# Value matmuls of the older unit ahead of the transposes of the newer one, in the units' loop of a hybrid decoder step

## What is computed

```python
# NSA mixer: three branches (compressed, selected, window), each a masked softmax attention
s = einsum('btghd,bngd->btghn', q, k) * scale
p = masked_softmax(s, mask)
o_branch = einsum('btghn,bngd->btghd', p, v)
o = g0 * o_cmp + g1 * o_slc + g2 * o_win
# DSA mixer: one branch, whose mask keeps the top-k keys of an indexer
o_d = einsum('btghk,btkgd->btghd', masked_softmax(q . k, top_k_mask), v)
# then both are gated, projected up, merged, projected out, added to x, and normed
```

## Time and profile before

| | |
|---|---|
| median of three runs | 699.51 us |
| the profiled execution: its own time | 697.51 us |
| its span, first to last instruction | 695.7 us |
| mean granted TensorE clock | 0.970 of full |
| PE busy over the span | 635.9 us (91%) |
| DVE busy over the span | 371.5 us (53%) |
| ACT busy over the span | 270.2 us (39%) |
| POOL busy over the span | 146.9 us (21%) |

### The profile page before, as it was taken

One profiled execution on the slowest core, in us unless ns is written; L12 is line 12 of the kernel. 1 busy time (PEld: TensorE's weight loads), 2 busy tenths in 40 slices (PEclk: granted clock), 3 DMA queues, 4 the chain that ended last, 5 costly groups with the idle time before them and its releaser, 6 DMA issues. The chain is left out here.

```text
span 695.7 us, 12691 instructions
## 1 busy us (share of the span) xinstructions
PE 635.9 (91%) x4400; PEld 498.4 (72%) x4400; DVE 371.5 (53%) x1001; ACT 270.2 (39%) x627; POOL 146.9 (21%) x216
## 2 busy tenths in 40 slices
PE   3979999998999978798989998999999999999990
PEld 1269676675776865464655667999999999987770
DVE  2044213969878358887787782444232623153536
ACT  5133233333231455666666672434222332221312
POOL 1013541260250434343434340000000000000001
PEclk9969999999999998999999999999999999999996
DMA  9943532322442352001300404235532324132003
GB/s 326 366 125 114 190 118 84 90 74 63 136 138 64 113 165 62 1 2 32 93 1 2 116 9 122 61 122 137 184 82 75 104 66 120 62 100 69 14 1 129
DMA packets 51807, 68.40 MB, mean 98 GB/s; under 512 B 5009, under 2 KB 34889, under 8 KB 51584
## 3 DMA queue, kind: packets, MB, share of 16 engines
q1 hardware_dynamic: 48496, 54.63, 26.3%
q10 hardware_dynamic: 1808, 6.31, 2.6%
q0 software_dynamic: 1440, 6.66, 2.4%
HBM read 62.99 MB, written 6.66 MB: 100 GB/s over the span
## 5 line engine op out<-in xcount | busy, mean ns | idle before, releaser
L1283 ACT ACTIVATE w_hi<-stage 128x1024 fp32r<-128x1024 f32 (+3 forms) x64 | 63.4, 990 | 195.5 <-PE psum L930 106.8
L1548 DVE TENSOR_TENSOR w_lo<-stage,w_hi 128x1024 fp32r<-128x1024 f32 x40 | 48.9, 1225 | 130.4 <-ACT w_hi L1283 127.0
L786 PE MATMUL psum<-w_hi,hT_hi 128*128 128x512 f32 (+7 forms) x240 | 84.7, 353 | 3.3 <-DVE hT_lo L1523 3.2
L788 PE MATMUL psum<-w_lo,hT_hi 128*128 128x512 f32 (+7 forms) x240 | 83.4, 348 | 0.0
L787 PE MATMUL psum<-w_hi,hT_lo 128*128 128x512 f32 (+7 forms) x240 | 83.3, 347 | 0.0
L762 POOL TENSOR_SCALAR prob<-prob,softmax_stats 128x31 f32<-128x31 f32 (+4 forms) x128 | 61.8, 496 | 86.5 <-DVE softmax_stats L1754 60.5
L711 POOL TENSOR_TENSOR w_lo<-stage,w_hi 128x1024 fp32r<-128x1024 f32 (+3 forms) x24 | 45.7, 1904 | 162.2 <-ACT w_hi L1283 162.2
L930 PE MATMUL psum<-hT_hi,w_hi 128*128 128x272 f32 x384 | 79.5, 288 | 0.0
L930 PE MATMUL psum<-hT_lo,w_hi 128*128 128x272 f32 x384 | 79.5, 288 | 0.0
L930 PE MATMUL psum<-hT_hi,w_lo 128*128 128x272 f32 x384 | 79.2, 288 | 0.0
L1416 ACT ACTIVATE prob<-psum,softmax_stats 128x31 f32<-128x31 f32 (+6 forms) x136 | 63.4, 466 | 26.1 <-DVE softmax_stats L1733 14.4
(11 more groups left out here) (295 smaller groups left out, 1132.0 us busy)
## 6 DMA issues: line engine op xcount, KB each, us to landing
stage<-in_w_in SPq DMA_DIRECT2D x14, 1024.0 KB, 5.1
stage<-in_w_ada SPq DMA_DIRECT2D x8, 1024.0 KB, 7.6
stage<-in_w_in SPq DMA_DIRECT2D x10, 512.0 KB, 5.3
stage<-in_w_out SPq DMA_DIRECT2D x4, 1024.0 KB, 5.0
staging<-in_x_prompt ACTq DMA_DIRECT2D x4, 512.0 KB, 5.8
qT_plain<-in_w_ada SPq DMA_DIRECT2D x2, 1024.0 KB, 10.8
qT_rot<-in_w_ada SPq DMA_DIRECT2D x2, 1024.0 KB, 12.3
cached<-in_cache_nsa_kv SPq DMA_DIRECT2D x32, 64.0 KB, 2.3
```

The costliest lines, as they stand in the source:

```text
L786: mm(out, left[0], right[0], start=first, stop=False, skip_group_check=True)
L788: return mm(out, left[0], right[1], start=False, stop=last, skip_group_check=True)
L1283: last = A(dst, src, ACT.Copy)
L1548: last = tt(dst, src, hi.bitcast(F32), ALU.subtract)
```

## The change

The two calls in the loop change places, so that turn i issues scores(i), values(i - 4), turn(i - 3). The two waits of `turn` for the copies of the unit before go, since values(i - 4), now ahead of it, waits for the same copies.

```diff
--- before.py
+++ after.py
@@ -1146,10 +1146,7 @@
                 src = prob[:, u % 4]
                 for g in range(2 if kind == "P" else 1):
                     pe.wait_ge(scaled, TURNS[u] + g + 1)
-                    if g and ORDP[u]:
-                        pe.wait_ge(pt_dve, ORDP[u])
-                    elif not g and ORD[u]:
-                        pe.wait_ge(pt_act, ORD[u])
+
                     if kind == "P" and b != CMP:
                         for n in range(unit[3] + 1):
                             last = pe.transpose(bank[4 + g][:, P * n:P * n + P], src[:, g, P * n:P * n + P], ident)
@@ -1219,10 +1216,10 @@
             for i in range(len(UNITS) + LAG + 3):
                 if i < len(UNITS):
                     scores(i)
+                if 0 <= i - LAG - 1 < len(UNITS):
+                    values(i - LAG - 1)
                 if 0 <= i - LAG < len(UNITS):
                     turn(i - LAG)
-                if 0 <= i - LAG - 1 < len(UNITS):
-                    values(i - LAG - 1)
                 turn_samples(i - LAG - 2)
```

## The result

The changed kernel takes 722.37 us (median of 4 runs, 715.99 to 725.16), against 699.87 us for the kernel before (4 runs). The ratio is 1.0317, with a 95% interval of 1.0241 to 1.0393. That is slower, as forecast, but by 22.5 us and not by 13.5, and above the range's upper end of 720.

What follows compares the result with a forecast made beforehand. TensorE leads the loop, VectorE and ScalarE close behind. Bare copies of 9.5 (NSA blocks), 1.1 (S units), 0.5 (DSA) and 2.5 us (loop's end) make 13.6; 697.51 becomes 711.1, and the median, 2.0 higher, 713; range 704 to 720.

Steps and rivals of the forecast that it cites:

- The move of the wait: TensorE's loop: the wait for copies isn't removed but moves from the transposes to the values, earlier by a set of values.
- The sum of bare copies: Loop: copy time with hand-overs beyond the covering scores, summed over units and the loop's end, 13.6 us.
- WIN t = 3 and t = 2: NSA blocks: loss where these units' copies outlast the scores four units later, 0.66 and 0.53 us.
- the loop's end: Last units, with no scores left to cover their copies: 2.5 us, less the wait already there.
- waits before scores: ScalarE's later copy delays the exponentials that scores wait for; this link stays shorter than the new turn: nothing.
- the clock's term: TensorE's granted clock in the loop: new gaps of at most 0.8 us each leave it unchanged; nothing in the sum.
- the stage behind the loop: After the loop: unchanged; the freed weight load moves with the loop's end and costs nothing.
- rival 3: Clock falls: small gaps bring half-speed stretches, each 1.2 us dearer; five more would give 719. Chance 0.11.
- the main case: Whole kernel: 13.6 us of bare copies, clock unchanged, giving 713 us. Chance 0.80.
- rival 1: Absorbed: loss falls where VectorE or ScalarE limits anyway; only the bare end, 2.5 us, counts: 702. Chance 0.06.
- rival 2: Faster: ending 1.9 us of copy waits, engines behind closing up as much again, copies covered: 695.7. Chance 0.03.
- low end of 704: Range's lower bound: no lag around the copies, so the sum falls to 4 us.

Runs made afterwards that it cites:

- e3: Changed kernel's order, but with values of unit i - 5, so copies have scores plus values as cover; within 1% of the kernel before.
- e7: Changed kernel with VectorE's bank 5 copy made twice for eight WIN units; 14.3 us more full-clock and 16.7 us more lost time than the kernel before.
- e2: Kernel before with values first only in the DSA units and the loop's end; 5.5 us more full-clock time, 2.6 us more lost time.
- e1: Kernel before with values first only in the NSA mixer's units; 8.2 us more full-clock time, 6.6 us more lost time.
- e9: Kernel before with TensorE waiting for copies straight behind the transposes in 16 DSA units; 15.2 us more full-clock time, 0.6 us more lost time.
- e13: Kernel before with TensorE waiting for copies behind the transposes in the 24 NSA units of j = 2 and 3; 25.7 us more lost time.
- e12: Kernel before with values first only for the last four units; 1.1 us more full-clock time, 3.5 us more lost time.
- e17: Kernel before with scores issued twice in the 24 NSA units of j = 2 and 3, no added wait; 0.7 us more lost time.
- e6: Kernel before with values first only in 31 units predicted as covered; 1.1% slower, 1.4 us more full-clock time, 6.6 us more lost time.
- e15: Kernel before with values first only for NSA units of j = 2 and 3; 7.5 us more full-clock time, 4.1 us less lost time.

## Why the prediction was right in part and wrong in size

**The move of the wait.** Right. The two waits vanished from the transposes, and the values wait in their place; e3 shows that the order as such is free when copies are covered, e7 that the gap is VectorE's copy.

**The sum of bare copies, 13.6 us.** Right in size. Full-clock time grew by 12.3 us (683.6 in ten runs against 671.3), idle time in the trace by 12.8. The single terms hold too: WIN t = 3 and t = 2 were 0.66 and 0.53, measured 0.59 and 0.46 in the bracket and exact as distances; the loop's end 2.5, measured 2.1. But the agreement of the sum is partly luck: waits before values and transposes for copies grew by 14.2 - 4.1 = 10.1 us in the profile's brackets (before it was 1.9 + 1.0 + 0.9 + 0.3), and of the rest 1.9 us are more waits before scores and 0.5 before `turn_samples`, which I had put at nothing. The waits before scores come with the new order in DSA: e2's trace has 12.3 us of them, e1's 10.5, the kernel before 10.5. That they come because the transposes reach ScalarE later by a set of values is likely, but no run tested it.

**"My new gaps are at most 0.8 us each, so by the rows the clock stays; the sum has nothing for it."** This is the step that failed: the clock's term, put at nothing, was 8.8 us of lost time (35.5 in ten runs against 26.7), which is the difference between 713 and 722. I had generalised from one row, the window at 377, where 1.1 us of idle time in 4 left the clock at 1.00. e9 shows that such a row can be true for one kind of stretch, and e13 that it is false for another, in the same loop; e12 shows that the new order of the last four units alone brings 3.5 us of it. Gaps of up to 1.17 us also came up where VectorE was late, beyond my 0.8, and the stage behind the loop, which I had called unchanged, begins at half speed. The page "TensorE: Matmul & The Clock Gate" of the Trainium skill, in its section "A second HAM failure mode: psum-queue depth-cycling", had warned that small idles between groups make the clock swing and cost throughput; e13 agrees with it and e9 doesn't. It deserved more than the 0.11 of rival 3, whose mechanism (half-speed stretches, 1.2 us dearer each, 719) is what happened on top of the main case (three new stretches in the profile, of 1.7 to 3.4 us of lost time each). I had also set the two as alternatives where they add.

**The other rivals.** Absorption (rival 1) didn't happen: idle time grew by nearly the sum. Nor did the gain (rival 2). My low end of 704 came from copies without a lag, which the 1.00 us from scores to values, 0.31 us more than the copy, excludes.

**What stays open.** What tells gaps that lower the clock from gaps that don't. The NSA units' sets differ from DSA's in having the narrow CMP sets between them, but no run here varied that alone, and the half-speed stretch at the loop's end (e12) stands behind DSA and S units. That the change's own gaps cause its lost time is supported by e13 against e17, and by e1 and e12, in which parts of the change bring parts of the loss; e6, with lost time and almost no bare gaps, and e15, with bare gaps and less lost time than before, don't fit, and both stay unexplained.

## What to carry to other kernels

When a producer's result must pass through another engine, look at what the waiting engine has to do between producing and consuming it; moving a consumer ahead by one piece of work takes that piece out of the cover, whatever wait vanishes in exchange. Price such a gap as copy plus both hand-overs, less the work in between. Then ask separately what gaps do to TensorE's clock, and compare kernels by span times clock and by lost time over several runs, as the two have different causes and very different scatter.

## What was not expected of the hardware

- The hand-over figures are stable to a few hundredths of a microsecond: c was 1.00 us at every undisturbed WIN, t = 3, with or without filler, and an extra copy of 0.69 us with its own hand-over lengthened the gap by 0.73.
- The same kernel's lost time varies from run to run by a standard deviation of 3.4 us, its full-clock time by 2.3. Most of the spread of the times is the clock.
- 14 us more of idle time in one stretch cost no clock time (e9: 0.6, error 1.4), while 12 us more by the same waits in another cost 26 us of lost time (e13), twice the price of the gaps themselves.
- In e13 the clock stayed at its 1.2 GHz level through 10 us in which TensorE was busy without a gap (415 to 425).
